# Results of a layer's last two expert blocks stay in SBUF and are added through a matrix of gate weights

## The reference

```python
x = x + g1 * (merged @ w_out[l])                       # mixer sub-layer
h2 = rms_norm(x, norm_ffn_w[l]) * (1.0 + sc2) + sh2
x = x + g2 * grouped_moe(h2, ...)                      # 16 experts, each token goes to 2
# grouped_moe: y[token] = sum over its 2 experts of gate * ((silu(h@w_gate) * (h@w_up)) @ w_down)
# next layer begins with
h = rms_norm(x, norm_mix_w[l]) * (1.0 + sc1) + sh1
proj = h @ w_in[l]
```

## Time and profile before

| | us |
|---|---|
| median of 3 runs | 1659.15 (1657.87 to 1662.56) |
| the profiled execution: its own time | 1661.03 |
| the profiled execution: its span | 1659.2 |
| TensorE busy in it | 1494.5 (90%) |
| VectorE busy | 648.4 (39%) |
| ScalarE busy | 322.3 (19%) |
| mean granted TensorE clock | 0.951 of full speed |

### The profile page before, as it was taken

The page is one execution under the profiler, slowest core; times in us unless marked ns, Lnnn a source line. Parts: engine busy times, 40 slices in busy tenths (PEclk is TensorE's granted clock), DMA queues, the critical chain, the costliest instruction groups (busy, mean ns, idle before and its releaser), DMA issues.

```text
span 1659.2 us, 18860 instructions
## 1 busy us (share of the span) xinstructions
PE 1494.5 (90%) x5871; PEld 677.1 (41%) x5872; DVE 648.4 (39%) x1596; ACT 322.3 (19%) x830; POOL 131.9 (8%) x199
## 2 busy tenths in 40 slices
PE   5999999989994999989679999999899668999993
PEld 2544445544442333333244444454444323333331
DVE  0546425557624121211244553365763421122123
ACT  3234311100011121211143342111000111112120
POOL 1100000000000010100120000000100010010001
PEclk8999999999996999999889999999999879999997
DMA  9951112277716699999864012126764379997895
GB/s 332 361 218 51 51 51 102 102 264 279 286 59 233 200 345 383 389 385 387 314 247 159 1 51 102 51 102 213 291 223 198 142 245 385 390 386 265 316 346 200
DMA packets 132684, 377.59 MB, mean 228 GB/s; under 512 B 12392, under 2 KB 14608, under 8 KB 132624
## 3 DMA queue, kind: packets, MB, share of 16 engines
q1 hardware_dynamic: 117440, 337.51, 54.9%
q0 software_dynamic: 6144, 20.98, 4.3%
q10 hardware_dynamic: 9040, 18.36, 3.0%
HBM read 345.88 MB, written 30.93 MB: 227 GB/s over the span
## 4 chain that ended last, share of the span: by engine, by line
PE 80%; DMA 9%; DVE 5%; ACT 2%; issue 2%; SPq 1%; POOL 0%; ACTq 0%; DVEq 0%; POOLq 0%
PE bank L1055 25%; PE bank L1300 18%; PE bank L1044 12%; PE bank L1312 8%; PE bank L1259 7%; DMA weight_ring<-in_w_up_dram 3%; PE bank L1292 2%; DMA regA<-in_w_up_dram 2%; DMA h_features<-in_ada_w_dram 1%; DMA expert_results<-merged_features 1%; DMA merged_features<-token_rows,regU 1%; PE bank L1123 1%; PE bank L1306 1%; PE bank L1112 1%; DMA regA<-expert_results,slot_index 1%
## 5 line engine op out<-in xcount | busy, mean ns | idle before, releaser
L1055 PE MATMUL bank<-h_features,weight_ring 128*128 128x512 f32 x768 | 346.0, 604 | 1.9 <-ACT regB L785 1.9
L1300 PE MATMUL bank<-weight_ring,merged_features 128*64 128x512 f32 x960 | 224.6, 622 | 15.4 <-DMA weight_ring<-in_w_up_dram 8.3
L1055 PEld LDWEIGHTS bank<-h_features,weight_ring 128*128 128x128 f32 x768 | 147.1, 194 | 184.5 <-issue 184.2
L1044 PE MATMUL bank<-weight_ring,h_features 128*128 128x512 f32 (+1 forms) x512 | 197.8, 544 | 0.0
L1915 DVE TENSOR_TENSOR merged_features<-bank,merged_features 64x512 f32<-64x512 f32 x44 | 30.5, 693 | 357.5 <-ACT merged_features L913 357.5
L1044 PEld LDWEIGHTS bank<-weight_ring,h_features 128*128 128x128 f32 x512 | 96.6, 192 | 95.0 <-issue 91.8
L1300 PEld LDWEIGHTS bank<-weight_ring,merged_features 128*64 128x64 f32 x960 | 73.8, 143 | 142.6 <-issue 137.8
L1300 PE MATMUL bank<-h_features,merged_features 128*64 128x512 f32 x256 | 117.0, 611 | 9.6 <-DMA regA<-in_w_up_dram 8.7
L1312 PE MATMUL bank<-weight_ring,merged_features 128*64 128x512 f32 x528 | 120.6, 598 | 1.6 <-DVE merged_features L1902 1.6
L1300 PE MATMUL bank<-regA,merged_features 128*64 128x512 f32 x256 | 117.4, 613 | 0.0
L1259 PE MATMUL bank<-weight_ring,merged_features 128*128 128x512 f32 x256 | 114.6, 602 | 3.0 <-POOL merged_features L649 3.0
(11 more groups left out here) (338 smaller groups left out, 1472.5 us busy)
## 6 DMA issues: line engine op xcount, KB each, us to landing
weight_ring<-in_w_gate_dram SPq DMA_DIRECT2D x22, 2048.0 KB
weight_ring<-in_w_up_dram SPq DMA_DIRECT2D x22, 2048.0 KB
weight_ring<-in_w_down_dram SPq DMA_DIRECT2D x22, 2048.0 KB
weight_ring<-in_w_in_dram SPq DMA_DIRECT2D x18, 2048.0 KB, 14.5
x_tokens<-in_ada_w_dram SPq DMA_DIRECT2D x14, 2048.0 KB, 7.9
h_features<-in_w_gate_dram SPq DMA_DIRECT2D x10, 2048.0 KB
regA<-in_w_up_dram SPq DMA_DIRECT2D x10, 2048.0 KB
regA<-in_ada_w_dram SPq DMA_DIRECT2D x8, 2048.0 KB, 8.4
```

Of the source, the lines that this page charges most:

```text
L1044: ins = te.matmul(bank[:, 0:w], hT[:, k, P * i:P * i + P], wv[:, k, :], start=(k == 0), stop=(k == KD - 1))
L1055: ins = te.matmul(bank[:, :], wv[:, k, c0:c0 + P], rhs[:, k, :], start=(k == 0), stop=(k == kn - 1))
L1300: ins = te.matmul(ps[3][64 * part:64 * part + 64, :], xT[:, k, :], w[:, k, :], start=(k == 0), stop=(k == KD - 1))
```

## The change

The results of a layer's last two blocks (numbers nb-2 and nb-1) are no longer stored to HBM. `y_row` puts them into two tiles in SBUF, `kept[0]` and `kept[1]`. At the start of the expert phase VectorE builds (`build_picks`) for each tile of tokens a 128 x 128 matrix that holds a token's gate weight at each row of the kept blocks that is one of its results and zero elsewhere, and the weights `wfar`, which are zero where a result is in a kept block. TensorE transposes the matrices and VectorE copies them to `pickT`. Behind the last `down`, TensorE multiplies them with the kept tiles (`kept_rows`: one matmul for each column half h, kept block a and token tile i, over 64 rows) into two banks a tile, and VectorE adds the banks to x (`near`).

All other results are gathered as before, but by one group of eight gathers in the order of the tiles, that waits only for the store of block nb-3, and into other buffers (`regB` and `mlstm_v_and_one` for k = 0). VectorE adds them (`far`) in an order written out by hand, mixed with `near`, the last `y_row`, and (between the layers) the first `h1_evac`.

Also moved: `param_columns` and `head_cols` of the next layer stand ahead of the last `down` and its `y_row`; `h1_transposes(1)` behind the first q group and `h1_transposes(3)` behind the first kv group, in both layers; `h1_evac(1)` to the end of ScalarE's and VectorE's stretch between the layers, and at the program's start behind the sines and cosines.

```diff
+kept = [mflat[:, 3584:4096], yb]
+picks = regU[:, 256:1024].rearrange("p (i n) -> p i n", i=NT)
+pick_part = [regP[:, 512 * k:512 * k + 512].rearrange("p (i a r) -> p i a r", i=NT, a=2) for k in range(2)]
+pickT = [regP[:, 512 * a:512 * a + 512] for a in range(2)]
...
-yg = [hT[:, :, :].rearrange("p a b -> p (a b)").rearrange("p (i d) -> p i d", i=NT), xn]
 vflat = vaug[:, :, :, :].rearrange("p a b c -> p (a b c)")
+yg = [[regB[:, D * i:D * i + D] for i in range(NT - 1)] + [vflat[:, 0:D]], [xn[:, i, :] for i in range(NT)]]
...
+kept_at = att[:, 0, 0:16].rearrange("p (a k i) -> p a k i", a=2, k=2)
+kept_from = att[:, 0, 16:17]
+wfar = att[:, 1, 0:8].rearrange("p (k i) -> p k i", k=2)
 ps = [ctx.enter_context(nc.psum_tensor(f"bank{b}", [P, 512], F32)) for b in range(8)]
+kept_bank = [ps[0:2], ps[2:4], ps[6:8], ps[0:2]]
...
-        for k in range(2):
-            wait_reg(pool, y_out, (nb if k else blocks_through(po, E - 2)) * 32 + 32)
-            for i in range(NT):
-                po.indirect_dma_start(out=yg[k][:, i, :], out_offset=None, in_=yd,
+        nb2 = po.value_load(tabs[0:1, 49:50], min_val=E - 2, max_val=MAXB - 2)
+        wait_reg(pool, y_out, nb2 * 32 + 32)
+        for i in range(NT):
+            for k in range(2):
+                po.indirect_dma_start(out=yg[k][i], out_offset=None, in_=yd,
                                       in_offset=bass.IndirectOffsetOnAxis(ap=slot_u[:, k, i:i + 1], axis=0)).then_inc(yg_in[k][i], 16)
...
     act.wait_ge(mod_ready, 1)
     h1_evac(0)
-    h1_evac(1)
     act.wait_ge(angles, 1)
     ac.activation(sinr[:, :, :].rearrange("p i f -> p (i f)"), rt[:, 64:96], ACT.Sin).then_inc(act_const, 1)
     ac.activation(cosr[:, :, :].rearrange("p i f -> p (i f)"), rt[:, 96:128], ACT.Sin).then_inc(act_const, 1)
+    h1_evac(1)
...
-        with act.Fori(0, nb1) as b:
+        with act.Fori(0, nb2) as b:
             act.wait_ge(gu_ready, b + 2)
             silu_()
             act.wait_ge(xt_ready, b + 3)
@@ -936,7 +947,12 @@
             act.wait_ge(ht_ready, b + 2)
             h_evac()
             store_rows(b)
-        store_rows(nb1)
+        act.wait_ge(gu_ready, nb)
+        silu_()
+        act.wait_ge(xt_ready, nb + 1)
+        xt_act()
+        act.wait_ge(ht_ready, nb)
+        h_evac()
...
-                if i >= 2:
-                    h1_evac(i - 2)
+                if i == 2:
+                    h1_evac(0)
             normalise(l + 1, NT - 1)
+            h1_evac(1)
...
         h1_transposes(0)
-        h1_transposes(1)
         for i in range(NT):
             pe.wait_ge(h1_low, i + 1)
             pe.wait_ge(h1_high, i + 1)
             token_group("q", i, 512)
             if i == 0:
+                h1_transposes(1)
                 h1_transposes(2)
+            token_group("kv", i, 256)
+            if i == 0:
                 h1_transposes(3)
-            token_group("kv", i, 256)
...
         gate_up(0)
         wait_reg(pe, xg_in[1], rows_before[1] + 16)
         x_transposes(1)
+        pe.wait_ge(picks_built, 1)
+        for a in range(2):
+            for i in range(NT):
+                ins = te.transpose(ps[a][:, P * i:P * i + P], picks[:, i, MB * a:MB * a + P], ident[:, :])
+        ins.then_inc(picks_turned, 1)
         h_transposes(0)
...
+        with pe.If(l < DEPTH - 1):
+            param_columns(l + 1)
         pe.wait_ge(ht_evac, nb)
         pe.wait_ge(y_taken, nb)
         last = (E - 1) % BUF
         wait_reg(pe, w_dn[last], (l + 1) * (HELD[last] * DN[last]))
         down(last)
-        with pe.If(l < DEPTH - 1):
-            param_columns(l + 1)
+        def kept_rows(i, a):
+            for h in range(2):
+                ins = te.matmul(kept_bank[i][h][:, :], pickT[(a + h) % 2][64 * h:64 * h + 64, P * i:P * i + P], kept[a][64 * h:64 * h + 64, :],
+                                start=(a == 0), stop=(a == 1))
+            if a == 1:
+                ins.then_inc(kept_ready, 1)
+        pe.wait_ge(picks_taken, 1)
+        kept_rows(0, 0)
+        kept_rows(1, 0)
+        pe.wait_ge(y_taken, nb + 1)
+        kept_rows(0, 1)
+        kept_rows(1, 1)
+        for i in (2, 3):
+            if i == 3:
+                pe.wait_ge(kept_read, 1)
+            kept_rows(i, 0)
+            kept_rows(i, 1)
         pe.sem_inc(moe_done, 1)
...
@@ -1425,7 +1468,6 @@
     start_layer(dve, 0)
     h1_evac(0)
-    h1_evac(1)
...
     ve.sem_inc(angles, 1)
+    h1_evac(1)
...
+        def y_row(to):
+            ve.tensor_tensor(to, ps[5][:, :], g2bc[:, :], ALU.mult).then_inc(y_taken, 1)
...
+        def build_picks():
+            ve.tensor_scalar(kept_from, cum[:, E - 1:E], float(MB), -2.0 * MB, ALU.mult, ALU.add).then_inc(picks_step, 1)
+            dve.wait_ge(picks_step, 1)
+            for k, at in enumerate((lo, hi)):
+                for a in range(2):
+                    ve.tensor_scalar(kept_at[:, a, k, :], at, kept_from, 1.0 + MB * a, ALU.subtract, ALU.subtract)
+                ins = ve.scalar_tensor_tensor(wfar[:, k, :], at, kept_from, wsel[:, k, :], ALU.is_le, ALU.mult)
+            ins.then_inc(picks_step, 1)
+            dve.wait_ge(picks_step, 2)
+            for k in range(2):
+                for i in range(NT):
+                    for a in range(2):
+                        ins = ve.tensor_scalar(pick_part[k][:, i, a, :], io64[:, :], kept_at[:, a, k, i:i + 1], wsel[:, k, i:i + 1],
+                                               ALU.is_equal, ALU.mult)
+            ins.then_inc(picks_step, 1)
+            dve.wait_ge(picks_step, 3)
+            ve.tensor_tensor(picks[:, :, 0:P].rearrange("p i (a r) -> p i a r", a=2), pick_part[0], pick_part[1], ALU.add)
+            ve.tensor_tensor(picks[:, :, P:P + MB], pick_part[0][:, :, 0, :], pick_part[1][:, :, 0, :], ALU.add).then_inc(picks_built, 1)
         ve.sem_inc(y_taken, 1)
         ve.sem_inc(y_out, 32)
         dve.wait_ge(xt_ready, 1)
         xt_dve()
+        build_picks()
         dve.wait_ge(sil_ready, 1)
-        ve.tensor_tensor(hx, ps[3][64:P, :], hsil[64:P, :], ALU.mult).then_inc(hx_ready, 1)
+        h_row()
         dve.wait_ge(xt_ready, 2)
         xt_dve()
-        with dve.Fori(0, nb1) as b:
+        dve.wait_ge(picks_turned, 1)
+        for a in range(2):
+            ins = ve.tensor_copy(pickT[a], ps[a][:, :])
+        ins.then_inc(picks_taken, 1)
+        with dve.Fori(0, nb2) as b:
...
-        dve.wait_ge(y_ready, nb)
-        dve.wait_ge(y_out, nb * 32)
-        y_row()
-        def combine(k, i):
+            y_row(yb)
+        dve.wait_ge(sil_ready, nb)
+        dve.wait_ge(ht_ready, nb1)
+        h_row()
+        dve.wait_ge(xt_ready, nb + 1)
+        xt_dve()
+        dve.wait_ge(y_ready, nb1)
+        y_row(kept[0])
+        def far(k, i):
             dve.wait_ge(yg_in[k][i], l * 16 + 16)
-            hlink(ve.scalar_tensor_tensor(xs[:, i, :], yg[k][:, i, :], wsel[:, k, i:i + 1], xs[:, i, :], ALU.mult, ALU.add))
+            hlink(ve.scalar_tensor_tensor(xs[:, i, :], yg[k][i], wfar[:, k, i:i + 1], xs[:, i, :], ALU.mult, ALU.add))
+        def near(i):
+            dve.wait_ge(kept_ready, i + 1)
+            for h in range(2):
+                ins = ve.tensor_tensor(xs[:, i, 512 * h:512 * h + 512], xs[:, i, 512 * h:512 * h + 512], kept_bank[i][h][:, :], ALU.add)
+            hlink(ins)
+            ve.sem_inc(kept_read, 1)
+        def last_row():
+            dve.wait_ge(y_ready, nb)
+            dve.wait_ge(y_out, nb2 * 32 + 32)
+            y_row(kept[1])
+        def whole():
+            ve.sem_inc(combined, 1)
         ve.sem_clear(head_step)
         with dve.If(l < DEPTH - 1):
             hn[0] = 0
             head_cols(l + 1)
             head_mod(modn[:, :])
-            for i in range(NT):
-                combine(0, i)
-            for i in range(NT):
-                combine(1, i)
-                ve.sem_inc(combined, 1)
+            far(0, 0)
+            far(1, 0)
+            last_row()
+            far(0, 1)
+            near(0)
+            whole()
+            near(1)
+            near(2)
+            far(1, 1)
+            whole()
+            near(3)
             start_layer(dve, l + 1)
             h1_evac(0)
+            for i in (2, 3):
+                far(0, i)
+                far(1, i)
+                whole()
             h1_evac(1)
...
-            for i in range(NT):
-                combine(0, i)
-            for i in range(NT):
-                combine(1, i)
-                ve.sem_inc(combined, 1)
+            far(0, 0)
+            far(1, 0)
+            last_row()
+            far(0, 1)
+            near(0)
+            whole()
+            far(1, 1)
+            near(1)
+            whole()
+            for i in (2, 3):
+                far(0, i)
+                far(1, i)
+                near(i)
+                whole()
```

22 lines of the change are left out of this document (12 added, 10 removed).

## The result

The change is slower: 1664.75 us, the median of 13 runs (1660.48 to 1668.35), against 1659.5 for the kernel before on the same chip (13 runs, 1650.93 to 1664.23). The ratio is 1.0041, with a 95% interval of 1.0027 to 1.0055, where 1655.3 us was forecast. The profiled execution took 1664.14, its span 1662.3; the mean granted clock was 0.953.

A forecast was written before the change was run, and what follows sets the result against it. TensorE, 80% of the chain, was taken as the bound, so only its gaps at layer ends could shorten. Terms -5.1 - 0.9 + 2.0 + 0.2 = -3.8 took the median from 1659.15 to 1655.3 us, range 1651.5 to 1660.5.

The forecast's parts named there:

- End of layer 1, -5.1: Behind layer 1's last down: without the store and its wait, last x whole at 1650.2, not 1655.33; -5.1 us.
- Rival 2: Both layer ends: gathers land late and hold up the last y_row and the additions behind it; 1657.7 us, chance 0.09.
- Between the layers, -0.9: Layer 0's end into layer 1: earlier q -2.8, moved transposes +0.9, low clock on q group +1.0; together -0.9 us.
- -2.8: Between the layers: layer 1's first q group starts at 839.5, not 842.33; -2.8 us.
- Start, +2.0: Program's start: tile 1's transposes come back behind q, +0.9, and q group slower by the clock, +1.1 us.
- rival 3: First q groups of both layers: low clock paid in full, +2.65 and +2.2 for 1.1 and 1.0; 1658.1 us, chance 0.14.
- Picks, +0.2: Start of the experts: build_picks, eight more transposes and copies mostly hidden; +0.1 us a layer, +0.2 in all.
- `kept_rows`: Behind the last down: pairs of 64-row matmuls run side by side on TensorE, 1.0 us a pair, 1.76 as bound.
- Rival 4: Both layer ends: kept_rows pairs don't overlap, 1.76 us each, making the kernel slower; 1662.4 us, chance 0.07.

The follow-up runs named there:

- e10: Changed kernel with the four gathers of tiles 0 and 1 sent at once, the other four only behind y_row(kept[0]); 1654.96 us, ratio 0.9984.
- e13: Changed kernel with ScalarE's h1_evac(0) ahead of square(2), gathers of tiles 2 and 3 behind y_row(kept[0]), and the program's start as before; 1644.67 us, ratio 0.9925.
- e7: Changed kernel with the last pass of ScalarE's and VectorE's block loops put back in the loop, decided by branches; 1664.21 us, ratio 1.0037.
- e14: Changed kernel with six gathers (tiles 0 to 2) sent at once and those of tile 3 behind y_row(kept[0]); 1658.23 us, ratio 1.0008.
- e11: Changed kernel with each of the eight gathers fetching 256 elements a row, not 1,024, so outputs are incomplete; 1668.38 us, ratio 1.0074.
- e6: Kernel before, with eight transposes of the identity (results unused) added ahead of h_transposes(0); 1657.68 us, ratio 0.9988.

## Why the prediction was wrong

- **End of layer 1, -5.1: this step failed.** It took it that the last `y_row` "starts at 1634.99 as before". Everything behind the last `down` came as worked out: 15.4 us to the last x (1643.62 to 1659.04, against 20.5). But what lies ahead grew by 5.9 us (row 15.1, not 9.2): some 4 for the late word, 2.0 for the last `down`, in part at the low clock. The whole is +0.2. The gathers started when it said, 2.7 us ahead of the last silu, and that was counted as slack. What eight of them, sent in a row, do to the two blocks still being computed was not looked for; e10 takes it away by sending four, and the end is then 5.8 shorter. Rival 2 asked for late gathers; it was their being under way early that cost.
- **Between the layers, -0.9: wrong by some 3.4 us.** q started 24.9 us behind the start of the last `down`, 2.9 sooner than before; -2.8 was said, and that step is right. But the last `down` came 0.9 later behind the last silu (6.3 us for 5.4), for here too `y_row` waited for TensorE's word: 4.7 us behind its `down`, not 3.7. The q group took 9.95, 2.1 more than before, where 1.0 was said and 2.2 was the bound. Not in the sum at all was the step of ScalarE and VectorE into layer 1's code, which the moved `h1_evac(1)` laid open. The opening took 4.5 us more for 1.9. From last silu to gates the two stretches give +2.5.
- **Start, +2.0: the number is right**, 2.3 (58.4 against 56.1), and e13 gets it back. Its terms are not: the q group took 9.88 us for 7.41, 2.5 more for the 1.1 said, and it started 1.0 sooner behind the first transposes (2.7 us for 3.6), where nothing was to be gained. That these two nearly cancel is luck. The two q groups paid nearly all that rival 3 gives them, 2.65 and 2.2.
- **Picks, +0.2: wrong in sign.** The eight transposes take their 1.1 us, and `gate_up` of block 1 behind them takes 7.09, not 9.88. The stretch of the first two blocks is 2.8 us shorter in layer 0 and 0.3 in layer 1 in the profiled pair.
- **`kept_rows`: right.** Three pairs took 2.80, 0.93 each for 1.0. Rival 4, the one slower case, is out; the kernel is slower by another mechanism.

The five stretches of the profiled pair sum to +2.2 and the span to +3.1, while the medians differ by 5.3 us and the ratio of all runs says about 6.8. The rest lies in untouched stretches or in how these two executions stand to their medians, and stays open. The moves' part is shown by time and not by stretches alone.

## What to carry to other kernels

Transfers that start earlier aren't free because nobody waits for them: ask which work is unfinished when they are in flight, and send ahead only those that the next step needs. A step is not hidden by the work it was written beside but by where each engine's list puts it; before moving one, look at what the moved engine does next, up to its branch. An operation brought forward on one engine pays only if the evacuations behind it, on every engine, are brought forward too.

## What the runs showed of the hardware

- With eight indirect gathers sent in a row from GpSimd, TensorE's semaphores reached VectorE up to 3.2 us late and ScalarE up to 4.3 (e7); with six up to 1.7 (e14), with four on time (e10). A quarter of the bytes made no difference (e11). The profile names the releaser "remote" or "another core or an unknown queue" there, though one core runs and no queue was awaited.
- VectorE's step into a new layer's code took 2.1 us with the DMA engines idle, and 2.8 to 5.6 us beside weight loads.
- Behind eight transposes in a gap, a group of 32 matmuls took 7.09 us (changed kernel) or 8.78 (e6), and 9.88 without them, at a granted clock of 1.00, 0.81 and 0.71.
